# Decode attention over cached pages: each page laid over 32 partitions, four positions to a partition, and the weights turned on VectorE in blocks of 32 by 32

## The reference

```python
def sb_attend(q, k, v, q_pos, k_pos, bias):
    z = jnp.einsum('bqhd,bkhd->bhqk', q, k) * (q.shape[-1] ** -0.5)
    z = z + bias[None, :, None, None]
    mask = k_pos[None, :] < q_pos[:, None]
    log_not = jnp.where(mask, jax.nn.log_sigmoid(-z), 0.0)
    suffix = lax.cumsum(log_not, axis=3, reverse=True) - log_not
    a = jnp.where(mask, jnp.exp(jax.nn.log_sigmoid(z) + suffix), 0.0)
    return jnp.einsum('bhqk,bkhd->bqhd', a, v)
```

## Time and profile before

| | us |
|---|---|
| three runs, median | 2755.46 |
| three runs, lowest and highest | 2750.58, 2759.26 |
| profiled execution, its own time | 2745.58 |
| profiled execution, span | 2743.5 |
| PE busy in the span | 1814.7 |
| DVE busy | 1276.4 |
| ACT busy | 497.6 |

### The profile page before, as it was taken

The page is one execution under the profiler, slowest core; times in us unless marked ns, Lnnn a source line. Parts: engine busy times, 40 slices in busy tenths (PEclk is TensorE's granted clock), DMA queues, the critical chain, the costliest instruction groups (busy, mean ns, idle before and its releaser), DMA issues.

```text
span 2743.5 us, 31504 instructions
## 1 busy us (share of the span) xinstructions
PE 1814.7 (66%) x10482; PEld 864.7 (32%) x10482; DVE 1276.4 (47%) x3210; ACT 497.6 (18%) x1061; POOL 1296.6 (47%) x1172
## 2 busy tenths in 40 slices
PE   6987687898965934787556666556665643364747
PEld 3443343343433412222233343333333310011212
DVE  1106664535354664644435354244342554664551
ACT  2112221101121100211122222222221200011121
POOL 0014634425545563645464542345235567876760
PEclk8998899999986965898878777767776766587878
DMA  6888958889968897999899999899899999999992
GB/s 210 279 263 308 388 182 337 312 302 368 396 241 293 314 359 270 367 355 398 340 347 380 383 342 343 322 397 355 316 350 356 361 402 386 384 405 405 346 375 79
DMA packets 338178, 913.48 MB, mean 333 GB/s; under 512 B 36865, under 2 KB 46242, under 8 KB 337378
## 3 DMA queue, kind: packets, MB, share of 16 engines
q0 software_dynamic: 160512, 580.99, 56.0%
q1 hardware_dynamic: 175250, 324.59, 33.2%
q10 hardware_dynamic: 2256, 5.90, 0.6%
HBM read 894.82 MB, written 16.52 MB: 332 GB/s over the span
## 4 chain that ended last, share of the span: by engine, by line
DMA 26%; PE 16%; POOL 8%; SPq 6%; issue 5%; DVE 4%; ACT 1%; DVEq 0%; ACTq 0%; POOLq 0%
DMA arena<-in_cache_v_dram 10%; POOL arena L2128 8%; DMA arena<-in_cache_k_dram 4%; SPq L2178 3%; PE ps L467 3%; SPq L2183 3%; PE ps L2117 3%; DMA arena<-in_peer_w_q_dram 3%; PE ps L794 2%; PE ps L1108 2%; DMA arena<-in_peer_u_dram,arena 2%; DMA arena<-in_peer_v_dram,arena 2%; PE ps L865 2%; DMA out_ret_sample_dram<-arena 2%; DMA arena<-in_w_in_dram 1%
## 5 line engine op out<-in xcount | busy, mean ns | idle before, releaser
L2128 POOL DMA_INDIRECT arena<-in_peer_u_dram,arena x544 | 615.3, 1131 | 994.2 <-PE ps L2117 804.8
L2038 DVE CUSTOM_DVE_ANT_0 arena<-arena 128x1024 f32<-128x1024 f32 x544 | 656.0, 1223 | 544.3 <-DMA arena<-in_peer_u_dram,arena 536.3
L467 PE MATMUL ps<-arena 128*128 128x512 f32 (+1 forms) x1472 | 686.9, 620 | 85.5 <-DMA arena<-in_peer_w_q_dram 30.9
L2128 POOL DMA_INDIRECT arena<-in_peer_v_dram,arena x544 | 640.6, 1178 | 202.9 <-issue 163.4
L467 PEld LDWEIGHTS ps<-arena 128*128 128x128 f32 (+1 forms) x1472 | 275.5, 193 | 471.0 <-issue 343.2
L2117 PE MATMUL ps<-arena 128*32 128x512 f32 x2176 | 322.3, 715 | 146.5 <-DMA arena<-in_peer_v_dram,arena 124.2
L794 PE MATMUL ps<-arena 128*128 128x128 f32 x1024 | 195.8, 353 | 209.5 <-DMA arena<-in_cache_k_dram 155.2
L794 PEld LDWEIGHTS ps<-arena 128*128 128x128 f32 x1024 | 154.8, 182 | 298.9 <-DMA arena<-in_cache_k_dram 158.5
L865 PE MATMUL ps<-arena 128*32 128x512 f32 x512 | 101.5, 876 | 152.6 <-DMA arena<-in_cache_v_dram 152.6
L1258 ACT ACTIVATE arena<-ps 128x512 f32<-128x512 f32 x256 | 143.4, 593 | 282.8 <-PE ps L794 282.5
L2117 PEld LDWEIGHTS ps<-arena 128*32 128x32 f32 x2176 | 71.5, 124 | 327.3 <-issue 300.9
(11 more groups left out here) (214 smaller groups left out, 1636.8 us busy)
## 6 DMA issues: line engine op xcount, KB each, us to landing
arena<-in_w_in_dram SPq DMA_DIRECT2D x156, 512.0 KB, 7.5
arena<-in_cache_k_dram SPq DMA_DIRECT2D x256, 256.0 KB
arena<-in_cache_v_dram SPq DMA_DIRECT2D x256, 256.0 KB
arena<-in_peer_w_q_dram SPq DMA_DIRECT2D x64, 512.0 KB, 12.6
arena<-in_w_out_dram SPq DMA_DIRECT2D x32, 512.0 KB, 10.1
arena<-in_w_b_up_dram SPq DMA_DIRECT2D x24, 512.0 KB, 6.6
arena<-h_for_experts POOLq DMA_DIRECT2D x80, 128.0 KB, 13.4
arena<-in_peer_u_dram,arena POOLq DMA_INDIRECT x544, 9.4
```

Source lines behind the costliest of these rows:

```text
L467: last = pe.matmul(bank[0:rows(t), :], x[:, c, cs], weight(pe, g.no, name, c), start=(c == 0), stop=(c == nd - 1))
L2038: dve.tensor_tensor_reduce(ring[j], ring[j], HREP[:, g, :], 1.0, 0.0, ALU.mult, ALU.add, A16[:, p, 4 * g + a:4 * g + a + 1]).then_inc(u_us ...
L2128: pool.indirect_dma_start(ring[j], None, table, bass.IndirectOffsetOnAxis(ap=IDX[:, i % 2, 4 * g + a:4 * g + a + 1], axis=0)).then_inc(row ...
```

## The change

Each page now goes to 32 partitions. Partition 32k + m of a buffer holds positions 4m to 4m + 3 of page k of the unit, side by side, 8 KB that are contiguous in DRAM too. So entry e of the buffer's second axis no longer is a page: it is every fourth position, from offset e, of all four pages.

- Keys: a turn of `KP[:, e, ...]` gives columns (k, m) for offset e. ACT puts them back into the order of the positions as it copies: column (e, n) of the bank goes to 4n + e, so each write steps over four elements. Scores and all that follows up to the exponential are as before.
- Weights: the exponential writes Ad in the order r, e, m in place of r, m, e. The turn is then one VectorE instruction on 128x512 that turns each block of 32 by 32 by itself: block (k, r, e) of Ad, rows 32k.. by 32 positions m, becomes rows 32k + m by the 32 head-and-token columns. In this layout that is what `weigh_values` needs against the new VP; its products and their number stay.
- PE's four transposes and ACT's copy of a period go. The turn writes AdT in SBUF, so bank 4 is no longer covered, and the waits on `w_kept` of its other users become waits on one another. The name `w_kept` now is the semaphore that orders show as d_weights_turned.
- DVE's turn stands in the period's unit r = 3 at 1.45, ahead of the logits at 1.6. It waits for the exponential (`w_put`) and, from the second period on, until PE has used all values of the period before (`values_used`), as ACT's copy had done.

The diff (code in the middle of functions; the lines marked "..." are left out between hunks):

```diff
@@ -587,8 +587,8 @@
             sem("dn_" + n) for n in ("scores", "logits", "ln", "argument", "weights", "turned", "kept"))
         z_put, z_ln, total_put, carry_full, carry_put, arg_put = (
             sem("d_" + n) for n in ("logits", "ln", "total", "carry", "carry_kept", "argument"))
-        w_put, w_turned, w_kept, values_used, o_copied, o_turned, o_kept = (
-            sem("d_" + n) for n in ("weights", "weights_turned", "weights_kept", "values_used", "o_copied", "o_turned", "o_kept"))
+        w_put, w_kept, values_used, o_copied, o_turned, o_kept = (
+            sem("d_" + n) for n in ("weights", "weights_turned", "values_used", "o_copied", "o_turned", "o_kept"))
         r_rot = sem("r_rotated")
         t_scores, t_q, t_k, t_state, t_root = (
             sem("t_" + n) for n in ("scores", "q_decayed", "k_decayed", "state", "root"))
...
@@ -809,7 +809,7 @@
 
             def new_scores(b):
                 if b:
-                    pe.wait_ge(w_kept, 2 * b - 1)
+                    pe.wait_ge(zn_put, b)
                 pe.wait_ge(q_block, 2 * b + 2)
                 for hp in range(HP):
                     last = pe.matmul(ps[0:NS, 4, 0:NS], Qb[:, b % 2, hp, :], KTs[:, hp, :], start=(hp == 0), stop=(hp == HP - 1))
...
@@ -818,14 +818,14 @@
             def new_weights(b):
                 pe.wait_ge(an_put, b + 1)
                 if b:
-                    pe.wait_ge(w_kept, 2 * b)
+                    pe.wait_ge(an_kept, b)
                 pe.transpose(ps[0:NS, 4, P:P + NS], An[0:NS, :], ident[0:NS, 0:NS]).then_inc(an_turned, 1)
 
             def carry(p):
                 m = p % 2
                 pe.wait_ge(total_put, p + 1)
                 if p:
-                    pe.wait_ge(w_kept, p)
+                    pe.wait_ge(carry_put, p)
                 if p + 1 < PERIODS:
                     if m:
                         pe.wait_ge(zn_put, (p + 1) // 2 + 1)
...
@@ -837,18 +837,6 @@
                 if m:
                     pe.matmul(ps[:, 4, 200:201], const("carry_all"), tot[:, 0:1], start=False, stop=False)
                 pe.matmul(ps[:, 4, 200:201], const("carry_in"), tot[:, m:m + 1], start=False, stop=True).then_inc(carry_full, 1)
-
-            def turn_weights(p):
-                b, m = p // 2, p % 2
-                pe.wait_ge(w_put, p + 1)
-                if m:
-                    if b + 1 < DECB:
-                        pe.wait_ge(zn_put, b + 2)
-                else:
-                    pe.wait_ge(an_kept, b + 1)
-                for r in range(4):
-                    last = pe.transpose(ps[:, 4, r * P:(r + 1) * P], Ad[:, r * P:(r + 1) * P], ident)
-                last.then_inc(w_turned, 1)
 
             def weigh_values(p, r):
                 b, m = p // 2, p % 2
...
@@ -868,7 +856,8 @@
 
             def turn_output(b):
                 pe.wait_ge(o_copied, b + 1)
-                pe.wait_ge(w_kept, min(2 * b + 3, PERIODS))
+                if b:
+                    pe.wait_ge(o_kept, 2 * b)
                 for hp in range(HP):
                     last = pe.matmul(ps[:, 4, 256 + 8 * hp:264 + 8 * hp], Od[:, hp * P:(hp + 1) * P],
                                      select[:, 8 * hp:8 * hp + 8], start=True, stop=True)
...
@@ -893,8 +882,6 @@
                     carry(p - 1)
                 if 2 <= p < PERIODS + 2:
                     weigh_values(p - 2, r)
-                if r == 3 and 1 <= p <= PERIODS:
-                    turn_weights(p - 1)
                 if u + 1 < 4 * PERIODS:
                     yield when(g.no, "D", u + 1.5)
                     turn_keys(u + 1, 1)
...
@@ -1255,7 +1242,8 @@
                     act.wait_ge(scores_done, i - 1)
                 for hp in (2 * half, 2 * half + 1):
                     act.wait_ge(keys_turned, HP * i + hp + 1)
-                    act.activation(KPT[:, i % 2, hp, :], ps[:, hp % 2, :], ACT.Copy).then_inc(keys_kept, 1)
+                    dst = KPT[:, i % 2, hp, :].rearrange("p (n e) -> p e n", e=4)
+                    act.activation(dst, ps[:, hp % 2, :].rearrange("p (e n) -> p e n", e=4), ACT.Copy).then_inc(keys_kept, 1)
 
             def softplus_parts(p):
                 act.wait_ge(z_put, p + 1)
...
@@ -1285,15 +1273,10 @@
             def weights(p):
                 act.wait_ge(arg_put, p + 1)
                 if p:
-                    act.wait_ge(w_turned, p)
+                    act.wait_ge(w_kept, p)
                 want_exp(act)
-                act.activation(Ad, Cd, ACT.Exp).then_inc(w_put, 1)
-
-            def keep_weights(p):
-                act.wait_ge(w_turned, p + 1)
-                if p:
-                    act.wait_ge(values_used, 4 * p)
-                act.activation(AdT.rearrange("p r n -> p (r n)"), ps[:, 4, :], ACT.Copy).then_inc(w_kept, 1)
+                dst = Ad.rearrange("p (r e m) -> p r m e", r=4, e=4)
+                act.activation(dst, Cd.rearrange("p (r m e) -> p r m e", r=4, e=4), ACT.Exp).then_inc(w_put, 1)
 
             def copy_output(b):
                 act.wait_ge(values_used, 8 * b + 8)
...
@@ -1315,8 +1298,6 @@
                     softplus_parts(p - 1)
                 if r == 1 and p < PERIODS and p % 2:
                     keep_new_weights(p // 2)
-                if r == 3 and 1 <= p <= PERIODS:
-                    keep_weights(p - 1)
                 if u + 1 < 4 * PERIODS:
                     keep_keys(u + 1, 0)
                 yield when(g.no, "D", u + 1.9)
...
@@ -1723,6 +1704,13 @@
                 dve.scalar_tensor_tensor(out=Cd, in0=Zd, scalar=tot[:, 3:4], in1=Cd, op0=ALU.subtract,
                                          op1=ALU.subtract).then_inc(arg_put, 1)
 
+            def turn_weights(p):
+
+                dve.wait_ge(w_put, p + 1)
+                if p:
+                    dve.wait_ge(values_used, 4 * p)
+                dve.transpose(AdT.rearrange("p r n -> p (r n)"), Ad).then_inc(w_kept, 1)
+
             def output(b):
                 dve.wait_ge(o_turned, b + 1)
                 for j in range(2):
...
@@ -1749,6 +1737,9 @@
                         arguments(p - 1)
                     if p < PERIODS and p % 2 == 0:
                         new_sums(p // 2)
+                if r == 3 and 1 <= p <= PERIODS:
+                    yield when(g.no, "D", u + 1.45)
+                    turn_weights(p - 1)
                 if r == 3 and p < PERIODS:
                     yield when(g.no, "D", u + 1.6)
                     logits(p)
...
@@ -2180,7 +2171,8 @@
                 def load_pages(cache, u, dst, landed):
                     pages = ins[cache][0].rearrange("n p h d -> n p (h d)")
                     for k in range(4):
-                        sp.dma_start(dst[:, k, :], pages[bass.ds(page(u // 4, u % 4, k), 1)].rearrange("a p d -> p (a d)")).then_inc(landed, 16)
+                        rows_ = pages[bass.ds(page(u // 4, u % 4, k), 1)].rearrange("a (m e) d -> (a m) (e d)", e=4)
+                        sp.dma_start(dst[32 * k:32 * k + 32].rearrange("p e d -> p (e d)"), rows_).then_inc(landed, 16)
 
                 def load_cache():
                     def keys(u):
```

## The result

The changed kernel takes 3049.6 us (median of 4 runs, 3047.8 to 3053.4) against 2753.0 for the kernel before on the same chip: 1.108 times as long, 95% interval 1.106 to 1.111. Its profiled execution took 3051.1 us with a span of 3049.0, 305.5 us more than the 2743.5 of before.

A forecast was written before the change was run, and what follows sets the result against it. Transfers were taken to bound the decode stage. Terms of 389 - 48 + 0 + 0 + 10 + 10 = +361 us on the span of 2743.5 gave 3104.5, stated as 3115 us for the kernel; range 2940 to 3390.

The forecast's parts named there:

- The page loads: Decode stage: 134.2 MB of pages, each load to 32 partitions, cost 2.9 us more per MB, +389 us.
- my two bounds: Page loads: 2.5 us per MB (half the rate) gives 335 us, 4.9 gives 658 us.
- the copies of the expert input: Transfers already in the trace, 128 KB each into 32 partitions, costing 2.9 to 4.9 us more per MB.
- The gaps: Decode stage: slower transfers fill part of the 97 us in which both queues wait, -48 us.
- Larger packets: Page loads: 8 KB packets in place of 2 KB save between 18 and 0 us, taken as 0.
- PE and ACT's lost work: Decode stage: 64 transposes and 16 copies go, -24 to 0 us, taken as 0.
- ACT's strided writes: Copies of turned keys write every fourth element: 0 to 107 us, taken as +10 us.
- DVE's turn and wait: Decode stage: 16 turns, 12 to 39 us, and their waits for values, 0 to 121 us; taken as +10 us.
- the first: Rival: loads to the two halves of the partitions overlap, +71 to +168 us, 2825 to 2925 us; chance 0.10.
- the second: Rival: the destination costs nothing, but ACT's strided copies and DVE's turn do, 2830 to 2980 us; chance 0.05.
- the third: Rival: not slower; 8 KB pages go at full rate and get more DMA time, 2715 us; chance 0.08.
- the one sign: Decode stage: PE's waits for keys and values in sum at least double from 290 us.

The follow-up runs named there:

- two experiments: The changed kernel with 2 KB packets into the same 32 partitions, 2995.8 us, and the changed kernel with pages to 64 partitions by 4 KB, 3018.3 us.
- the loads alone: A separate kernel that only loads pages, in 11 phases: 206 to 247 GB/s or 382 to 424 GB/s, by the partitions each load writes.
- the alternating order: The changed kernel with the four pages of a unit issued in the order 0, 2, 1, 3: 3044.6 us, ratio 1.107.

## Why the prediction was right

The time, 3049.6 us, lies in the range of 2940 to 3390, 65 us under the 3115 forecast, and slower was given 0.91. Step by step, with the stage of 1177 us and 312 MB (265 GB/s): at 401 GB/s they need 778 us. The share of 1.01 against 1.03 without gaps leaves about 23 us of gaps, so the low rate costs 376 us. The same reckoning of the stage of before is 768 us, about 50 of gaps (0.97 of 1.03) and 47 for what else is below 401, the input copies among it. The shares are given to 0.01, which is 9 to 11 us of such a stage, so the split between gaps and low rate is no sharper than that.

- **The page loads.** Forecast +389, measured about 376 - 47 = +329, or 2.45 us per MB of pages. That is close to the lower of my two bounds, half the rate (2.5), and in three stretches without a gap, of the changed kernel and of two experiments, twice the page bytes fill 95 to 98% of the time. Half is a round figure, though: reckoned in the same way the price is about 2.1 us per MB with 2 KB packets and 2.4 with 4 KB rows. I took 2.9 from the copies of the expert input, which reach as high as 4.9; they cost more than half the rate explains, and I did not find out why. This is the term that was mis-sized.
- **The gaps.** Forecast -48, measured about -27. I had set them at 97 us; by the share they were nearer to 50, and the rest was low rate. Half of them was a guess, and about half of the true ones went.
- **Larger packets.** I took 0 of -18. In the slow kernel they do not help: they cost, 54 us against 2 KB packets, and this cost is already inside the 329. With both halves written they are worth much more than the 18 us that I had allowed: 2766 against 2671. The error was to reckon only the rate of a packet, 401 against 411, and not the gaps, which went too.
- **PE and ACT's lost work, ACT's strided writes, DVE's turn and wait.** Forecast +20 in sum, measured +4 (-3 to +11) with all of them in place. Each by itself came out near its bounds: the copies at 1.11 us, a little over twice their time per element, where twice was my upper bound; the turn at 0.71 us, at the cheap end; its waits 69 us in 12 times, under the 121. None of it reached the end of the kernel.
- **The sum** is 329 - 27 + 4 = +306 where +361 was said, and 305.5 was measured. So close a fit is partly luck: 329 and -27 are a split of the growth of the stage itself (312 us, of which 10 are 4 MB more that fell into the longer stretch), not two measurements of their own. In the forecast, too, errors offset: 60 us too much for the loads, 21 too much taken off for the gaps, 16 too much for the rest.

Of the rivals, the first is refuted by the loads alone, by the alternating order and by the changed kernel's own 241 GB/s, the second by the kernel with all but the page loads, the third by the one with the page loads only. The mechanism of the third is borne out in part: pages with larger packets do take more of the DMA engines' time, and that made the one sign fail that I had named, PE's waits for pages, which were to double and did not (278 us against 290). The size of a loss does not say which engine will wait for it.

## What to carry to other kernels

In a stage bound by transfers, ask of each load which partitions it writes, not only how many bytes and how large the rows: here 32 partitions in a row, or 64 of one half, went at half the rate, and 32 with a step of four, which reach both halves, at all of it. Another transfer of the same form, already in the trace, shows the kind of cost and its direction; its size (2.9 to 4.9 us per MB here) can be well above what the new one pays (2.45), so keep the plain estimate, half the rate, beside it. When a layout makes one engine's write strided, look whether the engine can read with the stride instead.
